# Forming two of sixteen weight residuals per column tile by an accumulating GpSimd DMA instead of VectorE

## Chip, core and metric

One NeuronCore of a Trainium2 chip runs the whole program in one launch. The metric is device microseconds of that core, the median over runs.

## What is computed

One block of a streaming encoder for 256 tokens of width 2048, in float32: a SwiGLU feed-forward (FFN) part, a mixer (a gated linear recurrence beside causal pooling), and a second FFN part, each with an RMS norm before and after it. The change touches only the gate and up products of the two FFN parts:

```python
def swiglu(h, w_gate, w_up, w_down):
    return (jax.nn.silu(h @ w_gate) * (h @ w_up)) @ w_down

h = swiglu(rmsnorm(x, ffn1_pre_g[l]), ffn1_w_gate[l], ffn1_w_up[l], ffn1_w_down[l])
x = x + 0.5 * rmsnorm(h, ffn1_post_g[l])
```

w_gate and w_up are 2048 x 5632, w_down is 5632 x 2048.

## The kernel before, in words

Every product is made of three float32r products, so as to come near float32: an operand a is split into hi = a rounded to float32r, and lo = a - hi, and a·w is taken as a_hi·w_hi + a_hi·w_lo + a_lo·w_hi. These are the three matmuls of the helper `three` (lines 729 to 731). The activations stay on chip in both parts (`xT_hi`, `xT_lo`); the weights stream in once from HBM.

**The stream of weight halves.** A half is 128 x 1024 float32 (512 KB). All weights of the program are one numbered sequence of 640 halves. SP loads two halves (1 MB) at a time into one of four places of `raw` (line 170). For each half ScalarE rounds `raw` into `whi` (function `hi`, line 299), and VectorE subtracts that from `raw` into `wlo` (function `lo`, line 481). `whi` and `wlo` are rings of four halves. TensorE then runs twelve 512-column matmuls on the half (`narrow_half`, line 733).

**What orders it.** Each engine has its own program, written out by hand, and counting semaphores between them. `hi` of half g waits until TensorE is through with half g-4 (`w_used`), since they share a ring place. `lo` of half g waits for `hi_ready` of half g. TensorE waits for `lo_ready` of half g, which counts up in order, one for each half. SP refills a place of `raw` when `lo_ready` shows that both of its halves have been split. GpSimd's queue does small things only: inverse roots, constants for the mixer, and the loads of `gpost`, `gn_sb` and `wp_sb`.

**The column tiles.** The gate and up products of an FFN part are made in eleven column tiles of 512 columns, `up_tile` on each engine: halves 0 to 7 are the gate weights (one half is two 128-row chunks of 512 columns), halves 8 to 15 the up weights. Tile 0 is written out apart, tiles 1 to 10 are a hardware loop. In them ScalarE and VectorE work three halves ahead of TensorE (`AHEAD`). TensorE transposes the hidden tile made before it in front of half 3 (eight short matmuls, line 801), and ScalarE and VectorE split it at their step 4; ScalarE takes the silu of the gate columns at its step 8 (line 348), VectorE multiplies by the up columns behind step 15 (line 520). The down products, the mixer's input product and its output product use the same stream and are not changed.

Of the kernel before, what the change touches and what calls it, by code (L numbers as in the profile page):

```python
# [16 lines left out]
P = 128  # L17
# [4 lines left out]
NT = 512  # L22
# [10 lines left out]
RAW = 4  # L33
# [13 lines left out]
G_FFN1, G_MIX, G_FFN2, LB0, LB1, PSC = 0, 16, 32, 48, 56, 64  # L47
VROWS = 72
VEARLY = G_MIX


TB = (4, 5, 6)
# [3 lines left out]
def build(nc, x_d, g1pre_d, w1g_d, w1u_d, w1d_d, g1post_d, mixpre_d, win_d, lb_d, gnorm_d,  # L56
# [58 lines left out]
    with ExitStack() as ctx:  # L115
        ps = [ctx.enter_context(nc.psum_tensor(f"ps{i}", [P, NT], f32)) for i in range(8)]

        def sem(name):
            return ctx.enter_context(nc.semaphore(name))

        raw_in = [sem(f"raw_in{i}") for i in range(RAW)]
        hi_ready, lo_ready = sem("hi_ready"), sem("lo_ready")
        w_used = sem("w_used")
        x_in = [sem(f"x_in{i}") for i in range(DN)]
        vec_in, vrest_in, gain_in, mixw_in = sem("vec_in"), sem("vrest_in"), sem("gain_in"), sem("mixw_in")
        ident_ok, consts_ok = sem("ident_ok"), sem("consts_ok")
# [91 lines left out]
        def _(pool):  # L218
# [22 lines left out]
            def load_gain(b, gain):  # L241
                pool.wait_ge(w_used, b)
                pool.dma_start(gpost[:], gain[0:1, :].broadcast_to([P, D])).then_inc(gain_in, 16)

            inv_root(0, False)
            load_gain(D1, g1post_d)
            inv_root(1, True)

# [34 lines left out]
            load_gain(OUT, mixpost_d)  # L283
            inv_root(3, False)
            inv_root(4, False)
            load_gain(D2, g2post_d)
            inv_root(5, True)

# [2 lines left out]
        def _(act):  # L291
            def hi(g, j=0):

                if isinstance(j, int) and g + 16 * j >= END:
                    return
                act.wait_ge(raw_in[g // 2 % RAW], j * 32 + 16 * (g // 2 // RAW + 1))
                if not (isinstance(j, int) and g + 16 * j < RING):
                    act.wait_ge(w_used, j * 16 + (g - RING + 1))
                nc.scalar.activation(whi[:, g % RING, :], raw[:, g // 2 % RAW, 1024 * (g % 2):1024 * (g % 2 + 1)],  # L299
                                     ACT.Copy).then_inc(hi_ready, 1)  # L300

            squares = {x_sq: 0, y_sq: 0}
            before = []
# [31 lines left out]
            def up_tile(b, j):  # L335
                f, k, step = (0, 0, 0) if b == U1 else (1, 4, 2)
                first = isinstance(j, int)
                for h in range(16):
                    if first and 6 <= h < 6 + DN:
                        x_square(k, step, h - 6)  # L340
                    if not first and h == 4:
                        hidden_hi(f, j - 1)
                    if h == (13 if first else 8):
                        act.wait_ge(w_used, j * 16 + (b + 8))
                        if first:
                            act.wait_ge(r_ok, k + 1)
                        for t in range(TOK):
                            nc.scalar.activation(nat[:, t, :], ps[t][:], ACT.Silu,  # L348
                                                 scale=rr[:, k, t:t + 1]).then_inc(silu_ok, 1)
                    hi(b + h + AHEAD, j)  # L350
                    if first and h < KC // 2 - 2:
                        x_hi_part(step, G_FFN2 if f else G_FFN1, h + 2)

# [112 lines left out]
        def _(dve):  # L466
# [38 lines left out]
            def up_tile(b, j):  # L505
                f, k, step = (0, 0, 0) if b == U1 else (1, 4, 2)
                first = isinstance(j, int)
                for h in range(16):
                    if first and h == 11:
                        mean_square(k, x_sq, TOK * DN * (step + 1))  # L510
                    if not first and h == 4:
                        hidden_lo(f, j - 1)
                    lo(b + h + AHEAD, j)
                    if first:
                        x_after_half(step, 3, G_FFN2 if f else G_FFN1, h)

                dve.wait_ge(w_used, j * 16 + (b + 16))
                for t in range(TOK):
                    dve.wait_ge(silu_ok, j * 2 + (2 * FTILES * f + t + 1))
                    V.scalar_tensor_tensor(out=nat[:, t, :], in0=ps[2 + t][:], scalar=rr[:, k, t:t + 1],  # L520
                                           in1=nat[:, t, :], op0=ALU.mult, op1=ALU.mult).then_inc(h_ok, 1)
# [202 lines left out]
        def _(pe):  # L724
# [87 lines left out]
            def up_tile(b, j):  # L812
                f, step = (0, 0) if b == U1 else (1, 2)
                first = isinstance(j, int)
                for h in range(16):
                    if not first and h == 3:
                        hidden(f, j - 1)
                    if first and h < 8:
                        x_before_half(step, h)
                    if first and not f and h == 1:  # L820
                        n = VROWS - VEARLY
                        pe.wait_ge(vrest_in, 64)
                        nc.tensor.transpose(ps[3][:, 0:n], vrest[0:n, :], ident[0:n, 0:n]).then_inc(vcol_tr, 1)
                    if first and not f and h == 8:
                        pe.wait_ge(vcol_ok, 2)
                    if h == 0 and (f or not first):
                        pe.wait_ge(silu_ok, j * 2 + 2 * FTILES * f)
                    if h == 8 and (f or not first):
                        pe.wait_ge(h_ok, j * 2 + 2 * FTILES * f)
                    narrow_half(b + h, j, h % 8, ps[0:2] if h < 8 else ps[2:4])  # L830

            def up(b):
# [143 lines left out]
```

## Time and profile before

| what | value |
|---|---|
| median of 3 timed runs | 1878.26 us (1876.82 to 1879.6) |
| profiled execution, first to last instruction (span) | 1875.8 us |
| TensorE matmuls / weight loads busy | 98% / 81% of the span |
| VectorE / ScalarE / GpSimd busy | 51% / 43% / 3% |
| chain of work that ended last | 97% on TensorE |
| DMA | 344.68 MB, mean 184 GB/s |
| mean granted TensorE clock | 0.994 |

The profile gives the span of the execution it recorded, and no other time of it; the median of the timed runs lies 2.5 us above that span, which is taken as what lies around it. Names: PE is TensorE, PEld its weight loads, DVE VectorE, ACT ScalarE, POOL GpSimd, SP the engine that issues the loads. Matmuls overlap each other: one takes 0.39 us, and the next starts 0.23 us after it, so busy time is the time in which at least one is running. The granted clock is a share of 2.4 GHz.

### The profile page before, as it was taken

What the parts mean: (1) busy time and instruction counts of PE and PEld (TensorE: products, weight loads), DVE (VectorE), ACT (ScalarE), POOL (GpSimd) and SP (SyncE); (2) the same over time, 40 slices, a digit from 0 to 9 for tenths busy, and PEclk for the clock granted to TensorE, in tenths of its full rate; (3) what the DMA queues carried; (4) which work ended last, traced back from release to release, by engine and by line L of the source; (5) the groups of instructions that cost most, each with busy time, mean ns of one, the idle gap of its engine ahead of it and who ended that gap; (6) DMA issues with size and microseconds to landing.
All of it is one profiled execution on the core that took longest, in us unless ns stands there. A gap on an engine that the chain in (4) does not pass through costs nothing.

```text
span 1875.8 us, 21635 instructions
## 1 busy us (share of the span) xinstructions
PE 1837.3 (98%) x8386; PEld 1525.8 (81%) x8386; DVE 951.9 (51%) x965; ACT 804.5 (43%) x926; POOL 49.6 (3%) x110
## 2 busy tenths in 40 slices
PE   7999999999999999999999999999999999999997
PEld 6888888888788887788888877888888888788886
DVE  4544445544444444655745456445444544444544
ACT  5444444444433434643234445444444444433432
POOL 0000000000000000250000000000000000000000
PEclk9999999999999999999999999999999999999998
DMA  7665656556566656455443554555555655555552
GB/s 263 189 198 180 196 183 192 188 186 194 194 198 191 197 186 199 158 184 176 135 135 131 200 185 149 188 191 189 183 197 182 198 179 191 208 185 201 186 194 90
DMA packets 145438, 344.68 MB, mean 184 GB/s; under 512 B 5400, under 2 KB 5472, under 8 KB 145008
## 3 DMA queue, kind: packets, MB, share of 16 engines
q1 hardware_dynamic: 144544, 339.77, 55.4%
q0 software_dynamic: 736, 4.26, 0.6%
q8 instruction: 30, 0.49, 0.1%
q14 instruction: 16, 0.13, 0.0%
q10 hardware_dynamic: 112, 0.03, 0.0%
HBM read 341.94 MB, written 2.10 MB: 183 GB/s over the span
## 4 chain that ended last, share of the span: by engine, by line
PE 97%; DVE 1%; ACT 1%; POOL 0%; issue 0%; DMA 0%; DVEq 0%; SPq 0%; POOLq 0%; ACTq 0%; PEldq 0%
PE ps L729 31%; PE ps L731 31%; PE ps L730 31%; PE ps L801 1%; PE ps L891 1%; PE ps L783 1%; DVE x L562 0%; PE ps L928 0%; ACT ps L311 0%; DMA x<-in_x_dram 0%; POOL hrr L282 0%; PE ps L918 0%; PE ps L879 0%; DVE xT_lo L488 0%; ACT xT_hi L318 0%
## 5 line engine op out<-in xcount | busy, mean ns | idle before, releaser
L481 DVE TENSOR_TENSOR wlo<-raw,whi 128x1024 fp32r<-128x1024 f32 x640 | 783.0, 1226 | 844.3 <-ACT whi L299 840.3
L299 ACT ACTIVATE whi<-raw 128x1024 fp32r<-128x1024 f32 x640 | 677.7, 1060 | 919.8 <-PE ps L731 918.8
L729 PE MATMUL ps<-whi,xT_hi 128*128 128x512 f32 x1728 | 680.5, 394 | 6.7 <-DVE wlo L481 4.4
L731 PE MATMUL ps<-whi,xT_lo 128*128 128x512 f32 x1728 | 674.9, 391 | 0.0
L730 PE MATMUL ps<-wlo,xT_hi 128*128 128x512 f32 x1728 | 674.6, 390 | 0.0
L729 PEld LDWEIGHTS ps<-whi,xT_hi 128*128 128x128 f32 x1728 | 325.8, 189 | 73.8 <-issue 4.8
L731 PEld LDWEIGHTS ps<-whi,xT_lo 128*128 128x128 f32 x1728 | 325.7, 188 | 68.7
L730 PEld LDWEIGHTS ps<-wlo,xT_hi 128*128 128x128 f32 x1728 | 326.1, 189 | 66.1
L729 PE MATMUL ps<-whi,hT_hi 128*128 128x512 f32 x832 | 324.5, 390 | 2.0 <-PEq L936 1.6
L731 PE MATMUL ps<-whi,hT_lo 128*128 128x512 f32 x832 | 323.7, 389 | 0.0
L730 PE MATMUL ps<-wlo,hT_hi 128*128 128x512 f32 x832 | 323.7, 389 | 0.0
L729 PEld LDWEIGHTS ps<-whi,hT_hi 128*128 128x128 f32 x832 | 156.2, 188 | 36.4 <-DVE yg L534 2.3
L731 PEld LDWEIGHTS ps<-whi,hT_lo 128*128 128x128 f32 x832 | 156.2, 188 | 32.7
L730 PEld LDWEIGHTS ps<-wlo,hT_hi 128*128 128x128 f32 x832 | 156.2, 188 | 31.9
L348 ACT ACTIVATE nat<-ps,rr 128x512 f32<-128x512 f32 x44 | 27.9, 686 | 33.2 <-PE ps L731 33.2
L520 DVE SCALAR_TENSOR_TENSOR nat<-ps,rr,nat 128x512 f32<-128x512 f32 x44 | 31.0, 747 | 10.8 <-PE ps L731 10.8
L318 ACT ACTIVATE xT_hi<-ps,vcol 128x256 fp32r<-128x256 f32 x48 | 19.9, 472 | 36.5 <-PE ps L783 36.5
L488 DVE SCALAR_TENSOR_TENSOR xT_lo<-ps,vcol,xT_hi 128x256 fp32r<-128x256 f32 x48 | 20.8, 478 | 23.3 <-ACT xT_hi L318 23.3
L801 PE MATMUL ps<-ident,nat 128*128 128x128 f32 x208 | 27.0, 273 | 3.2 <-DVE nat L520 3.2
L801 PEld LDWEIGHTS ps<-ident,nat 128*128 128x128 f32 x208 | 24.1, 140 | 7.2 <-DVE nat L520 4.1
L501 DVE TENSOR_TENSOR hT_lo<-ps,hT_hi 128x512 f32 (+1 forms) x44 | 28.2, 682 | 2.8 <-ACT hT_hi L332 2.8
L783 PE MATMUL ps<-ident,x 128*128 128x128 f32 x96 | 16.0, 301 | 11.9 <-DVE x L562 8.6
(99 smaller groups left out, 365.7 us busy)
## 6 DMA issues: line engine op xcount, KB each, us to landing
raw<-in_ffn_w_gate_dram SPq DMA_DIRECT2D x88, 1024.0 KB, 5.2
raw<-in_ffn_w_up_dram SPq DMA_DIRECT2D x88, 1024.0 KB, 5.2
raw<-in_ffn_w_down_dram SPq DMA_DIRECT2D x88, 1024.0 KB, 5.2
raw<-in_w_in_dram SPq DMA_DIRECT2D x40, 1024.0 KB, 5.1
raw<-in_w_out_dram SPq DMA_DIRECT2D x16, 1024.0 KB, 4.9
x<-in_x_dram SPq DMA_DIRECT2D x4, 512.0 KB, 9.3
gpost<-in_ffn_post_g_dram POOLq DMA_DIRECT2D x2, 1024.0 KB, 5.0
out_dram<-x SPq DMA_DIRECT2D x4, 512.0 KB, 2.9
```

The source lines that it names most:

```text
L299: nc.scalar.activation(whi[:, g % RING, :], raw[:, g // 2 % RAW, 1024 * (g % 2):1024 * (g % 2 + 1)], ACT.Copy).then_inc(hi_ready, 1)
L318: ins = nc.scalar.activation(xT_hi[:, k, :], ps[TB[s % 3]][:, c * SEQ:(c + 1) * SEQ], ACT.Copy, scale=vcol[:, g0 + k:g0 + k + 1])
L348: nc.scalar.activation(nat[:, t, :], ps[t][:], ACT.Silu, scale=rr[:, k, t:t + 1]).then_inc(silu_ok, 1)
L481: V.tensor_tensor(wlo[:, g % RING, :], raw[:, g // 2 % RAW, 1024 * (g % 2):1024 * (g % 2 + 1)], whi[:, g % RING, :].bitcast(f32), ALU.subt ...
L488: ins = V.scalar_tensor_tensor(out=xT_lo[:, k, :], in0=ps[TB[s % 3]][:, c * SEQ:(c + 1) * SEQ], scalar=vcol[:, g0 + k:g0 + k + 1], in1=xT_ ...
L501: V.tensor_tensor(flat(hT_lo[:, bass.ds(j * 4 + 2 * c, 2), :]), ps[4 + c][:], flat(hT_hi[:, bass.ds(j * 4 + 2 * c, 2), :]).bitcast(f32), A ...
L520: V.scalar_tensor_tensor(out=nat[:, t, :], in0=ps[2 + t][:], scalar=rr[:, k, t:t + 1], in1=nat[:, t, :], op0=ALU.mult, op1=ALU.mult).then_ ...
L729: mm(bank, a_hi, whi[:, s, c0:c0 + NT], start=start, stop=False)
L730: mm(bank, a_hi, wlo[:, s, c0:c0 + NT], start=False, stop=False)
L731: return mm(bank, a_lo, whi[:, s, c0:c0 + NT], start=False, stop=stop)
L783: ins = nc.tensor.transpose(ps[TB[s % 3]][:, c * SEQ + t * P:c * SEQ + (t + 1) * P], x[:, t, k * P:(k + 1) * P], ident[:])
L801: ins = nc.tensor.transpose(ps[banks[c]][:, q * SEQ + t * P:q * SEQ + (t + 1) * P], src[:, t, n:n + P], ident[:])
```

## The change

In tiles 1 to 10 of both FFN parts halves 5 (gate) and 13 (up) get their lo part in another way. ScalarE, having rounded `raw` into `whi`, also writes the negative of the rounded value into `wlo` (a second ACTIVATE of the same size, scale -1). GpSimd waits for that (`neg_ok`) and issues a DMA that reads the same 512 KB of weights from HBM once more and adds them to `wlo` where they land (`accum_op`). VectorE does nothing on these halves but keep the count: it waits for `neg_ok` and for its own earlier count, and adds one to `lo_ready`. TensorE waits for the DMA (`acc_in`) in front of these halves. That is 2 halves x 10 tiles x 2 parts = 40 halves of 640.

```diff
+BY_DMA = (5, 13)
...
+            def residual_halves(b, wg, wu):
+                f = 0 if b == U1 else 1
+                for j in range(1, FTILES):
+                    for m, (h, w) in enumerate(zip(BY_DMA, (wg, wu))):
+                        c = 2 * (h % 8)
+                        rows = w[0].rearrange("(c p) f -> p c f", p=P)
+                        dst = wlo[:, (b + h) % RING, :].rearrange("p (c f) -> p c f", c=2)
+                        pool.wait_ge(neg_ok, j * 2 + (2 * (FTILES - 1) * f + m - 1))
+                        pool.dma_start(dst, rows[:, c:c + 2, bass.ds(j * NT, NT)],
+                                       accum_op=ALU.add).then_inc(acc_in, 16)
+
             inv_root(0, False)
+            residual_halves(U1, w1g_d, w1u_d)
             load_gain(D1, g1post_d)
...
             inv_root(4, False)
+            residual_halves(U2, w2g_d, w2u_d)
...
+            def hi_and_minus(g, j):
+
+                hi(g, j)
+                nc.scalar.activation(wlo[:, g % RING, :], raw[:, g // 2 % RAW, 1024 * (g % 2):1024 * (g % 2 + 1)],
+                                     ACT.Copy, scale=-1.0).then_inc(neg_ok, 1)
...
-                    hi(b + h + AHEAD, j)
+                    if not first and h + AHEAD in BY_DMA:
+                        hi_and_minus(b + h + AHEAD, j)
+                    else:
+                        hi(b + h + AHEAD, j)
...
-                    lo(b + h + AHEAD, j)
+                    if not first and h + AHEAD in BY_DMA:
+                        m = BY_DMA.index(h + AHEAD)
+                        dve.wait_ge(neg_ok, j * 2 + (2 * (FTILES - 1) * f + m - 1))
+                        dve.wait_ge(lo_ready, j * 16 + (b + h + AHEAD))
+                        dve.sem_inc(lo_ready, 1)
+                    else:
+                        lo(b + h + AHEAD, j)
...
+                    if not first and h in BY_DMA:
+                        pe.wait_ge(acc_in, j * 32 + (32 * (FTILES - 1) * f + 16 * BY_DMA.index(h) - 16))
                     narrow_half(b + h, j, h % 8, ps[0:2] if h < 8 else ps[2:4])
```

Two places of the programs that result. First ScalarE in the column loop, around the rounding of half 13. Before (line 299 is `hi`):

```order
L298 REGISTER_ALU [waits raw_in2]
L299 ACTIVATE whi<-raw 128x1024 [waits w_used]
L298 REGISTER_ALU [waits raw_in3]
L299 ACTIVATE whi<-raw 128x1024 [waits w_used]
```

After (line 316 is `hi`, line 322 the negative):

```order
L315 REGISTER_ALU [waits raw_in2]
L316 ACTIVATE whi<-raw 128x1024 [waits w_used]
L322 ACTIVATE wlo<-raw 128x1024
L315 REGISTER_ALU [waits raw_in3]
L316 ACTIVATE whi<-raw 128x1024 [waits w_used]
```

The second ACTIVATE stands between the rounding of half 13 and that of half 14; all else keeps its place. Second TensorE in the same loop, at the seam between half 4 and half 5 (lines 761 to 763 are the three matmuls of `three`). Before:

```order
L729 MATMUL ps<-whi,xT_hi 128x512
L730 MATMUL ps<-wlo,xT_hi 128x512
L731 MATMUL ps<-whi,xT_lo 128x512
L735 REGISTER_ALU
L729 MATMUL ps<-whi,xT_hi 128x512 [waits lo_ready]
L730 MATMUL ps<-wlo,xT_hi 128x512
```

After:

```order
L761 MATMUL ps<-whi,xT_hi 128x512
L762 MATMUL ps<-wlo,xT_hi 128x512
L763 MATMUL ps<-whi,xT_lo 128x512
L863 ISA
L767 REGISTER_ALU [waits acc_in]
L761 MATMUL ps<-whi,xT_hi 128x512 [waits lo_ready]
L762 MATMUL ps<-wlo,xT_hi 128x512
```

A wait for the DMA now stands in front of the half's first matmul, beside the old one for `lo_ready`. On GpSimd the 20 DMAs of each FFN part stand one behind another, each with its wait, and nothing but them until the load of `gpost`:

```order
L239 TENSOR_TENSOR rr<-ms,mhalf 128x2 [waits ms_ok,gp]
L257 DMA wlo<-in_ffn_w_gate_dram 128x2x512 [waits neg_ok]
L257 DMA wlo<-in_ffn_w_up_dram 128x2x512 [waits neg_ok]
L257 DMA wlo<-in_ffn_w_gate_dram 128x2x512 [waits neg_ok]
L257 DMA wlo<-in_ffn_w_up_dram 128x2x512 [waits neg_ok]
```

Where the root (line 239) was followed by the load of `gpost`, the accumulating DMAs now stand between them.

## Rows read from the trace of the kernel before

**Rows 1.** The page, part 1: busy us, share of the span, instructions.

```profile
PE 1837.3 (98%) x8386; PEld 1525.8 (81%) x8386; DVE 951.9 (51%) x965; ACT 804.5 (43%) x926; POOL 49.6 (3%) x110
```

**Rows 2.** Waits of PE: engine, line <- releaser: us in total, times, longest us.

```profile
PE ps L729 <- DVE wlo L481: 4.4, 1, 4.4
...
PE ps L801 <- DVE nat L520: 3.2, 2, 1.6
```

**Rows 3.** Windows, column tiles 1 to 10: us, busy (x) by engine, clock, DMA share, GB/s.

```profile
100.00:500.00 400.00, 400.00 (x1802) 331.93 (x1802) 199.13 (x180) 171.94 (x180) 0.00 (x0) 1.00 0.59 189
```

**Rows 4.** Lines by form: busy us, mean ns, idle before and its releaser.

```profile
L481 DVE TENSOR_TENSOR wlo<-raw,whi 128x1024 fp32r<-128x1024 f32 x640 | 783.0, 1226 | 844.3 <-ACT whi L299 840.3 <-DMA gpost<-in_ffn_post_g_dram 2.2 <-DVE T L618 0.3
...
L299 ACT ACTIVATE whi<-raw 128x1024 fp32r<-128x1024 f32 x640 | 677.7, 1060 | 919.8 <-PE ps L731 918.8 <-DMA raw<-in_ffn_w_gate_dram 0.8
```

**Rows 5.** Timeline of ACT, halves 5 and 6: start us, us, what, idle before.

```profile
288.84 1.06 ACT L299 ACTIVATE whi<-raw 128x1024 fp32r<-128x1024 f32 x1 [1.66 <-PE ps L731]
291.56 1.06 ACT L299 ACTIVATE whi<-raw 128x1024 fp32r<-128x1024 f32 x1 [1.66 <-PE ps L731]
```

**Rows 6.** Timeline of ACT, halves 13 and 14.

```profile
311.49 1.06 ACT L299 ACTIVATE whi<-raw 128x1024 fp32r<-128x1024 f32 x1 [1.66 <-PE ps L731]
314.21 1.06 ACT L299 ACTIVATE whi<-raw 128x1024 fp32r<-128x1024 f32 x1 [1.66 <-PE ps L731]
```

**Rows 7.** Timeline of PE: half 5's first, two within half 11, half 13's first.

```profile
297.69 0.39 PE L729 MATMUL ps<-whi,xT_hi 128*128 128x512 f32 x1
...
314.46 0.39 PE L731 MATMUL ps<-whi,xT_lo 128*128 128x512 f32 x1
314.69 0.39 PE L729 MATMUL ps<-whi,xT_hi 128*128 128x512 f32 x1
...
319.45 0.39 PE L729 MATMUL ps<-whi,xT_hi 128*128 128x512 f32 x1
```

**Rows 8.** Timeline of SP's queue: refills of raw after halves 5 and 13.

```profile
291.18 0.37 SPq L170 DMA_DIRECT2D raw<-in_ffn_w_up_dram  x1
...
313.97 0.37 SPq L170 DMA_DIRECT2D raw<-in_ffn_w_gate_dram  x1
```

**Rows 9.** DMA issues: line, op, xcount, KB each, median us to landing.

```profile
raw<-in_ffn_w_gate_dram SPq DMA_DIRECT2D x88, 1024.0 KB, 5.2
...
gpost<-in_ffn_post_g_dram POOLq DMA_DIRECT2D x2, 1024.0 KB, 5.0
...
wp_sb<-in_w_pool_dram POOLq DMA_DIRECT2D x1, 1024.0 KB, 6.1
...
gn_sb<-in_hgrn_g_norm_dram POOLq DMA_DIRECT2D x1, 64.0 KB, 3.4
```

**Rows 10.** Windows around the refill issued at 313.97 (columns as in rows 3).

```profile
314.40:314.90 0.50, 0.50 (x3) 0.40 (x3) 0.00 (x0) 0.50 (x1) 0.00 (x0) 1.00 0.00 0
314.90:315.40 0.50, 0.50 (x4) 0.40 (x3) 0.10 (x1) 0.37 (x1) 0.00 (x0) 1.00 1.24 98
...
318.40:318.90 0.50, 0.50 (x4) 0.42 (x3) 0.50 (x1) 0.00 (x0) 0.00 (x0) 1.00 0.26 98
318.90:319.40 0.50, 0.50 (x4) 0.42 (x3) 0.35 (x1) 0.00 (x0) 0.00 (x0) 1.00 0.00 0
```

**Rows 11.** Timeline of PE: two gaps outside the column loops.

```profile
507.10 1.09 PE L801 MATMUL ps<-ident,nat 128*128 128x128 f32 x8 [1.61 <-DVE nat L520]
...
752.53 1.27 PE L783 MATMUL ps<-ident,x 128*128 128x128 f32 x8 [4.46 <-DVE x L562]
```

**Rows 12.** Windows right behind these two gaps.

```profile
755.00:756.00 1.00, 0.98 (x2) 0.83 (x3) 1.00 (x3) 0.73 (x1) 0.00 (x0) 0.50 1.03 389
507.00:508.00 1.00, 0.90 (x9) 0.90 (x9) 0.04 (x1) 0.21 (x1) 0.00 (x0) 1.00 0.86 176
```

**Rows 13.** Chain of waits behind the second gap: start us, us, what.

```profile
758.37 0.43 PE ps L730
758.80 0.43 PE ps L731
```

More of the change, by code:

```diff
@@ L123, in build @@
         w_used = sem("w_used")
+        neg_ok, acc_in = sem("neg_ok"), sem("acc_in")
         x_in = [sem(f"x_in{i}") for i in range(DN)]
```

## The prediction

> **What bounds the kernel now.** I read the busy shares first. TensorE runs matmuls for 98% of the span, VectorE is at 51%, ScalarE at 43% [rows 1]. The 400 us stretch that holds most of the first part's column tiles shows the same more sharply: TensorE is busy for 400.00 of 400.00 us, at the full granted clock, while VectorE works for 199 us of it [rows 3]. The waits say so from the other side. In the whole program TensorE waited once for a lo part, 4.4 us, when the stream started, and its next wait for VectorE is the hidden tile at the two ends of the up products, 3.2 us in sum [rows 2]; neither is in the part changed here. So in the loop that the change edits nothing ever arrives late at TensorE. VectorE's idle time ahead of the lo subtraction, 844 us, ends almost always with ScalarE's rounding, and ScalarE's 920 us ends with TensorE giving a ring place free [rows 4]: both helpers are paced by TensorE, and their idle time is slack.
>
> The question is therefore not what the change takes off VectorE. It is how much slack the lo part of a half has, and whether the new way of making it fits in.
>
> **The slack of the two halves.** ScalarE starts rounding half 13 at 311.49 and half 14 at 314.21 [rows 6]; the step of 2.72 us is TensorE's time for one half. TensorE begins half 13 at 319.45 [rows 7]. For half 5 the two times are 288.84 [rows 5] and 297.69 [rows 7]; this one has 0.9 us more, since TensorE does its eight transposes in between. So the time from the rounding's start to the use is 7.96 us for half 13 and 8.85 us for half 5. Today rounding (1.06) and subtraction (1.23) take about 2.3 us of it [rows 4].
>
> **What is removed.** 40 subtractions of 1.226 us [rows 4], 49 us of VectorE's time. All of it lies beside matmuls, so it is worth nothing on the path: TensorE is the cover, and it does not idle there.
>
> **What is added on ScalarE.** 40 ACTIVATEs of the same size as the rounding, 1.06 us each, 42 us [rows 4]. The negative of half 13 starts when the rounding ends, at 312.55, and ends at 313.61; half 14 is rounded from 314.21 on, so 0.6 us is left [rows 6]. For half 5 it ends at 290.96, ahead of 291.56 [rows 5]. The idle time of 1.66 us before each rounding hides it; without that cover it would delay the next half's parts, which themselves have over 5 us of slack. Cost: nothing.
>
> **What is added on VectorE and moved on SP's queue.** Two waits and a count, no data. VectorE gets to the next subtraction long before ScalarE has rounded that half. The count for half 13 now comes at 313.6, where the subtraction had it ready just ahead of the refill of `raw` at 313.97; for half 5 the refill stood at 291.18, the count now comes at 290.96 [rows 8]. So the refill goes out some 0.2 to 0.3 us earlier, and at the same moment as the new DMA. The refill itself isn't needed until ScalarE rounds the same place's next halves, seven halves after half 13 was rounded, 17 us after the issue, against 5.2 us to land [rows 9]. Even a landing twice as late is hidden.
>
> **What is added on GpSimd.** Its queue does nothing in these stretches (0.00 busy in 400 us) [rows 3], so no DMA there waits behind another, and what stands behind them, the load of `gpost`, has its own wait for the end of the up products. Cost: nothing.
>
> **The added wait, which is the price.** TensorE may not start half 13 until the accumulating DMA has landed. What is queued behind that wait is every later matmul. The DMA goes out at about 313.61 and TensorE wants it at 319.45, so it has 5.8 us; for half 5, from 290.96 to 297.69, 6.7 us [rows 5 to 7]. No row shows a DMA that adds. The nearest rows: the smallest copy that GpSimd issues, 64 KB, lands 3.4 us after the issue; its copies of 1 MB land after 5.0 us (long rows) and 6.1 us (1 KB rows); SP's 1 MB in the same 2 KB rows as here after 5.2 us [rows 9]. So a plain copy of 512 KB, alone, would come in between 3.4 and 5.2 us, in time for both.
>
> But it is neither plain nor alone. The refill goes out with it. Alone, the refill moves no data for its first 1.0 us, then moves for 3.6 us (314.9 to 318.5) at a DMA share near 1, and lands 0.6 us later [rows 10, 9]. While it moves, the 16 DMA engines are full, so the two share them. The new DMA has 256 rows of 2 KB, the refill 512; taken in turns, the new one is through when 256 rows of each have gone. And an addition in place has to fetch two inputs for each row, the weights and what lies in `wlo`; I count its rows double. That makes 0.5 MB of refill and 1 MB for the addition, 1.5 times 3.6 = 5.4 us of moving. Landing: 1.0 + 5.4 + 0.6 = **7.0 us** after the issue.
>
> The bounds: 3.4 us from below (the smallest copy), and 9.7 us from above, the slowest copy of 1 MB, 6.1 us, behind a whole refill, 3.6 us. I take 7.0, which is near neither end but is the one that counts the work.
>
> The Trainium skill (Collectives: The Full Stack, "The bandwidth ceiling: the fold count and why AG ≠ RS ≠ AR") says that a reducing DMA runs at half a copy's rate, because it needs two source reads and not because of the addition; no run so far shows that here. By it the sum would stay as it is.
>
> **The sum.** Half 13: 313.61 + 7.0 - 319.45 = 1.16 us late, times 20 = 23 us. Half 5: 290.96 + 7.0 - 297.69 = 0.27 us, times 20 = 5 us. A late half is not caught up: the ring ahead is measured from TensorE's own progress, so each tile pays again. Together 28 us on the span of 1875.8, that is 1904; the median of the runs lies 2.5 us above the span, so **1906 us**. At the upper bound, 9.7 us, the halves are 3.86 and 2.97 us late, 137 us in all, and the time is 2015.
>
> **The rivals.** Changes of under 0.2%, 3.8 us here, can't be told from none by a measurement of this kernel.
>
> *The DMA lands in time* (not slower). The mechanism: the addition costs no more engine time than a copy. Then the moving takes 0.5 MB + 0.5 MB, 3.6 us, and the landing comes after 5.2 us, ahead of 5.8. It decides at 5.8 us; up to 6.0 the loss stays under 3.8 us. Time 1878, between 1876 and 1882. For it: copies of twice the size land in 4.6 to 5.2 us mostly alone. Against it: the second input and the refill that always goes out together with it. The skill's fit for DMAs that GpSimd issues (DMA: Bandwidth & Descriptors, "Anatomy of one DMA — SWDGE (gpsimd) path"), 2.0 us plus the bytes at 436 GB/s, makes 3.2 us by estimate for 512 KB. By it this rival would win; the rows for 1 MB, 5.0 and 6.1 us against its 4.4 [rows 9], say that it is low here even without an addition.
>
> *The addition is much slower than two reads* (over 9.7 us). If each row costs four times a copy's: 2 MB + 0.5 MB, 9.0 us of moving, landing after 10.6 us; halves 4.8 and 3.9 us late, 173 us. On top the clock: behind a gap of 1.61 us TensorE kept its full clock, behind one of 4.46 us it was granted half [rows 11, 12], and matmuls then stepped by 0.43 instead of 0.23 us [rows 13, 7] for some 5 us, which loses up to 2.6 us each time, 50 to 100 us. Time 2100 to 2150. For it: nothing in this trace bounds the pace of an addition.
>
> *TensorE speeds up* (faster). It steps by 0.227 us (2.72 over twelve matmuls) where 512 columns at 2.4 GHz need 0.213. If that difference were VectorE's traffic beside it, 40 halves of 12 matmuls would gain 6.6 us: 1872. Against it: in a window with VectorE at 0.00 [rows 10] it still steps by 0.23 us [rows 7], and ScalarE gets nearly the same traffic in exchange.
>
> That the change doesn't happen is out: the 40 DMAs stand in GpSimd's program.
>
> **How the numbers follow.** A landing between 6.0 and 9.7 us, the forecast: 0.62. In time: 0.20; I don't make it less, since 5.8 us and my 7.0 lie close and the sharing is argued, not seen. Over 9.7 us: 0.15. Faster: 0.03. So faster 0.03, same 0.20, slower 0.77. The range goes from 1876, the in-time case, to 2015, the upper bound; what it leaves out is the slow addition and the faster case, under 0.2.
>
> **What would show it.** In the profile after, VectorE's busy time falls by 49 us and ScalarE's rises by 42. TensorE's waits get a new row, on the DMA into `wlo`, 20 to 40 times, about 28 us, longest near 1.2 us, and more before half 13 than before half 5. The list of DMA issues gets 40 of 512 KB with a landing near 7 us, and the refill beside them lands later than 5.2 us. The clock stays at 1.00 in the loops. I am wrong if the landing is under 5.8 us or the wait row is missing; wrong in size if the landing is past 9 us; and wrong in mechanism if TensorE waits for anything else there.

## The result, and the profile after

| what | before | after |
|---|---|---|
| median of 4 timed runs each | 1878.93 us | 1992.96 us (1990.8 to 1994.52) |
| span of the profiled execution | 1875.8 us | 1992.8 us |
| mean granted TensorE clock | 0.994 | 0.982 |

The ratio is 1.061, with a 95% interval from 1.060 to 1.062. The kernel is 114 us slower. The forecast was 1906 us with a range from 1876 to 2015. The sign was right, and so was the place of the loss, a DMA that lands late in front of halves 5 and 13. The size was not, 28 us against 114, and two parts of the loss, the fall of the clock and the restart behind each gap, were not in the forecast at all.

Two lines of the page of the changed kernel, to be set against [rows 1]: busy times, and the DMA queue that GpSimd feeds (packets, MB, share of 16 engines' span).

```profile
PE 1873.5 (94%) x8386; PEld 1540.7 (77%) x8386; DVE 903.0 (45%) x925; ACT 842.1 (42%) x966; POOL 97.8 (5%) x150
...
q0 software_dynamic: 11616, 25.23, 6.4%
```

VectorE lost the 49 us that were taken off it (951.9 to 903.0), ScalarE got 38 us more. TensorE does the same matmuls and is busy 36 us longer, which the forecast had nowhere. GpSimd's queue of DMAs moved 21 MB more (it had 4.26 MB).

The waits of TensorE, against [rows 2] (engine, line <- releaser: us in total, times, longest us):

```profile
PE ps L761 <- DMA wlo<-in_ffn_w_up_dram: 34.1, 13, 3.3
PE ps L761 <- DMA wlo<-in_ffn_w_gate_dram: 30.4, 20, 2.0
PE ps L761 <- DVE wlo L507: 21.2, 8, 4.4
```

The first two rows are new. The third had 4.4 us before; the other 16.8 us are the same gaps, put down to VectorE's last subtraction where the profile couldn't place the DMA. Together the gaps make 30.4 + 34.1 + 16.8 = 81.3 us. With the 36.2 us of busy time that is 117.5, and the span grew by 117.0. So the whole loss is there. Idle time is not all of the lateness, though: the last matmul before a gap still runs for 0.39 us, where the next would have started 0.23 us after it. So a half is 0.16 us later than its idle time says, 88 us over the 40 gaps; the other 6.4 us of it are counted as busy time.

The landings, against [rows 9] (KB each, median us from issue to landing):

```profile
raw<-in_ffn_w_gate_dram SPq DMA_DIRECT2D x88, 1024.0 KB, 5.3
...
wlo<-in_ffn_w_gate_dram POOLq DMA_DIRECT2D x20, 512.0 KB, 8.1
wlo<-in_ffn_w_up_dram POOLq DMA_DIRECT2D x20, 512.0 KB, 8.2
```

The addition lands 8.1 to 8.2 us after its issue, and not after 7.0. The gate row of `raw` is a median over 88 loads, of which only 20 go out beside an addition, so it doesn't say what the refill pays. The loads that do go out beside one, taken one by one in the first part, land after 5.6 us behind half 5 and 5.7 us behind half 13 (medians of ten), where the same loads took 5.2 and 5.15 us before: 0.4 to 0.6 us later.

One half 13 from its rounding to its use, from the timelines of ScalarE, GpSimd, SP's queue and TensorE (start us, us, what, idle before):

```profile
343.85 1.06 ACT L316 ACTIVATE whi<-raw 128x1024 fp32r<-128x1024 f32 x1 [1.66 <-PE ps L763]
344.82 1.04 ACT L322 ACTIVATE wlo<-raw 128x1024 fp32r<-128x1024 f32 x1
...
346.16 1.20 POOL L257 DMA_DIRECT2D wlo<-in_ffn_w_up_dram  x1 [23.06 <-ACT wlo L322]
...
346.11 6.04 SPq L174 DMA_DIRECT2D raw<-in_ffn_w_gate_dram  x2
...
354.46 0.49 PE L761 MATMUL ps<-whi,xT_hi 128*128 128x512 f32 x1 [2.48 <-DMA wlo<-in_ffn_w_up_dram]
```

ScalarE starts the rounding at 343.85, so TensorE wants the half 7.96 us later, at 351.81. The negative is done at 344.82 + 1.04 = 345.86. GpSimd's DMA starts at 346.16, 0.30 us later; the refill had gone out at 346.11 (its row joins two issues, the second at 351.8). TensorE starts at 354.46, 2.65 us late, of which 2.48 us are idle. Half 5 of the same tile is 1.5 us late in the same way (wanted at 328.43, started at 329.93). Over all 40 the lateness is 2.7 us in front of half 13 and 1.7 us in front of half 5.

What the DMA engines did in that stretch, in windows (columns as in [rows 3]; the last two numbers are the DMA share and the GB/s):

```profile
349.40:349.90 0.50, 0.50 (x4) 0.42 (x3) 0.00 (x0) 0.50 (x1) 0.00 (x0) 1.00 1.04 406
349.90:350.40 0.50, 0.50 (x4) 0.42 (x3) 0.01 (x1) 0.45 (x1) 0.00 (x0) 1.00 1.04 369
...
351.40:351.90 0.50, 0.50 (x3) 0.15 (x1) 0.21 (x1) 0.00 (x0) 0.00 (x0) 1.00 1.19 221
351.90:352.40 0.50, 0.07 (x1) 0.00 (x0) 0.00 (x0) 0.39 (x1) 0.00 (x0) 1.00 1.09 201
...
352.90:353.40 0.50, 0.00 (x0) 0.00 (x0) 0.30 (x1) 0.17 (x1) 0.00 (x0) 1.00 1.13 209
```

At 349.4 to 350.4 the engines move data at the pace of a plain load, 369 to 406 GB/s. By 350.9 the 1 MB of the refill is through: the eight windows from 346.9 to 350.9, not all shown, add up to 0.98 MB. Then come 2 us at 201 to 221 GB/s with the engines just as full. That is the addition, at half the pace. The queues settle whose data it is: q1 is the one that SP feeds, q0 GpSimd's (packets, MB, share of the engines). First the refill's landing, then 350.1 to 350.9, then 351.9 to 352.9:

```profile
raw<-in_ffn_w_gate_dram SPq DMA_DIRECT2D x1, 1024.0 KB, 5.7
```

```profile
q1 hardware_dynamic: 131, 0.27, 97.1%
```

```profile
q0 software_dynamic: 99, 0.20, 110.1%
```

In the first of these stretches every packet is the refill's, in the second every one is the addition's. The first packet of the addition starts 4.7 us after its issue (4.6 us for half 5, medians of 20). So in the changed kernel the two transfers weren't served in turns: the refill went first, and the addition used the engines after it.

### The profile page after: what moved, and what is told of

The parts are those of the page before. It is cut to its first block, busy times and chain, and to the rows that moved or that the text cites. A ratio compares the mean times of both kernels' runs of the same rounds, so it can differ in the third digit from the quotient of the medians.

```text
span 1992.8 us, 21735 instructions
## 1 busy us (share of the span) xinstructions
PE 1873.5 (94%) x8386; PEld 1540.7 (77%) x8386; DVE 903.0 (45%) x925; ACT 842.1 (42%) x966; POOL 97.8 (5%) x150
## 4 chain that ended last, share of the span: by engine, by line
PE 79%; DMA 14%; ACT 3%; issue 3%; DVE 2%; POOL 0%; DVEq 0%; SPq 0%; POOLq 0%; ACTq 0%; PEldq 0%
PE ps L761 26%; PE ps L763 25%; PE ps L762 25%; DMA wlo<-in_ffn_w_gate_dram 8%; DMA wlo<-in_ffn_w_up_dram 5%; ACT wlo L322 2%; PE ps L925 1%; PE ps L815 1%; DVE wlo L507 1%; ACT whi L316 0%; DVE x L594 0%; PE ps L833 0%; PE ps L962 0%; ACT ps L334 0%; DMA x<-in_x_dram 0%
## 5 line engine op out<-in xcount | busy, mean ns | idle before, releaser
L507 DVE TENSOR_TENSOR wlo<-raw,whi 128x1024 fp32r<-128x1024 f32 x600 | 734.0, 1226 | 1009.1 <-ACT whi L316 1005.3
L761 PE MATMUL ps<-whi,xT_hi 128*128 128x512 f32 x1728 | 694.4, 402 | 87.7 <-DMA wlo<-in_ffn_w_up_dram 34.1
L763 PE MATMUL ps<-whi,xT_lo 128*128 128x512 f32 x1728 | 684.9, 396 | 0.0
L762 PE MATMUL ps<-wlo,xT_hi 128*128 128x512 f32 x1728 | 684.5, 396 | 0.0
L761 PEld LDWEIGHTS ps<-whi,xT_hi 128*128 128x128 f32 x1728 | 331.2, 192 | 172.4 <-DVE wlo L507 56.5
L763 PEld LDWEIGHTS ps<-whi,xT_lo 128*128 128x128 f32 x1728 | 331.2, 192 | 71.1
L762 PEld LDWEIGHTS ps<-wlo,xT_hi 128*128 128x128 f32 x1728 | 331.8, 192 | 67.2
L257 POOL DMA_DIRECT2D wlo<-in_ffn_w_gate_dram x20 | 24.3, 1216 | 479.2 <-ACT wlo L322 479.2
L257 POOL DMA_DIRECT2D wlo<-in_ffn_w_up_dram x20 | 24.1, 1203 | 468.2 <-ACT wlo L322 468.2
L322 ACT ACTIVATE wlo<-raw 128x1024 fp32r<-128x1024 f32 x40 | 41.6, 1041 | 0.0
```

What stands on the lines that cost most here:

```text
L257: pool.dma_start(dst, rows[:, c:c + 2, bass.ds(j * NT, NT)], accum_op=ALU.add).then_inc(acc_in, 16)
L322: nc.scalar.activation(wlo[:, g % RING, :], raw[:, g // 2 % RAW, 1024 * (g % 2):1024 * (g % 2 + 1)], ACT.Copy, scale=-1.0).then_inc(neg_ok, 1)
L507: V.tensor_tensor(wlo[:, g % RING, :], raw[:, g // 2 % RAW, 1024 * (g % 2):1024 * (g % 2 + 1)], whi[:, g % RING, :].bitcast(f32), ALU.subt ...
L761: mm(bank, a_hi, whi[:, s, c0:c0 + NT], start=start, stop=False)
L762: mm(bank, a_hi, wlo[:, s, c0:c0 + NT], start=False, stop=False)
L763: return mm(bank, a_lo, whi[:, s, c0:c0 + NT], start=False, stop=stop)
```

## Experiments

The theory from this profile was A: the addition waits for the refill that goes out beside it, and its late landing is the whole loss, directly and by the clock. The rival was B: an accumulating DMA takes some 5 us from issue to first data whatever runs beside it. A second rival was that the added traffic or ScalarE's added work slow the loop by themselves.

**The refill held back.** SP's refills that would go out beside an addition wait for it, 38 of the 40; the two behind half 13 of the last tile of each part are not held (the loop over tiles is written out for it):

```diff
+                if hold:
+                    sp.wait_ge(acc_in, 16 * hold)
                 dst = raw[:, n % RAW, :].rearrange("p (c f) -> p c f", c=chunks)
                 sp.dma_start(dst, src).then_inc(raw_in[n % RAW], 16)
```

> The changed kernel, but SP waits with the refill of raw that would go out beside each accumulating DMA until that DMA has landed (38 of the 40). In the changed kernel the DMA lands 8.1 us after its issue and moves data only in the last 3. Theory A (the refill's packets are served first, and the addition starts when they are through): the landing falls to about 5 us (1.2 us to start, 3 us of data, 0.6), TensorE's waits for it vanish, time about 1880. Theory B (an accumulating DMA needs some 5 us from its issue to its first data, whatever runs beside it): the landing stays near 8 us and the time near 1993.

Measured: 1897.99 us, ratio 1.011 (1.009 to 1.013). The list of DMA issues, the gate row:

```profile
wlo<-in_ffn_w_gate_dram POOLq DMA_DIRECT2D x20, 512.0 KB, 6.0
```

The landing fell from 8.1 to 6.0 us, so B is out as it was stated, and 95 of the 114 us went with it. But it is 6.0 and not the 5 that A gave. The windows behind a DMA issued at 316.72 show where the rest lies:

```profile
317.72:318.22 0.50, 0.50 (x4) 0.42 (x3) 0.00 (x0) 0.48 (x1) 0.20 (x1) 1.00 0.00 0
...
318.72:319.22 0.50, 0.50 (x4) 0.39 (x3) 0.50 (x1) 0.00 (x0) 0.00 (x0) 1.00 1.01 98
...
320.72:321.22 0.50, 0.50 (x4) 0.41 (x3) 0.27 (x1) 0.20 (x1) 0.00 (x0) 1.00 1.11 205
...
321.72:322.22 0.50, 0.50 (x4) 0.35 (x2) 0.46 (x1) 0.00 (x0) 0.00 (x0) 1.00 0.41 70
```

No data until 318.2, then 1.7 us in which the pace climbs, then 205 GB/s at a full DMA share to about 321.9, landing at 322.7. The addition's first packet starts 1.9 us after the issue, where the refill's data started after 1.0 us [rows 8, 10]. So A is right about the refill, and some of B is true too: the addition by itself is slower to begin and moves at half a load's pace. Of the 20 us that are left, 5.9 are the idle time of the two gaps whose refill wasn't held (3.5 and 2.5 us); no other gap in front of half 13 is over 0.54 us.

**Halves 4 and 12 in place of 5 and 13.** The refills then go out half a step away from the additions:

```diff
-BY_DMA = (5, 13)
+BY_DMA = (4, 12)
```

> The changed kernel with halves 4 and 12 in place of 5 and 13. The place in the ring and the slack are the same (7.96 us and 8.85 us), but the refill goes out 2.7 us before the addition instead of beside it, and the next one 2.7 us after it. Theory A: the addition waits for the rest of one refill only, lands after 5 to 6 us, little or no waiting, 1880 to 1895. Theory B: landing near 8 us, time near 1993.

Measured: 1901.77 us, ratio 1.013 (1.011 to 1.014).

```profile
wlo<-in_ffn_w_gate_dram POOLq DMA_DIRECT2D x20, 512.0 KB, 5.9
wlo<-in_ffn_w_up_dram POOLq DMA_DIRECT2D x20, 512.0 KB, 6.4
```

5.9 and 6.4 us without any wait added on SP: just moving the addition away from the refill's issue does nearly as much as holding the refill. The upper end of A's range was 1895; the time is 7 us above it. The addition alone was underrated here as well, and the one for half 12 has a refill 1.4 us ahead of it, so that its first packet starts 2.9 us after its issue and not 1.9. One gap, in the last tile of the first part, is 2.8 us long and has a fall of the clock behind it.

**A plain copy in its place, refill beside it.** The residual of these halves is left out of the computation.

```diff
-                        pool.dma_start(dst, rows[:, c:c + 2, bass.ds(j * NT, NT)],
-                                       accum_op=ALU.add).then_inc(acc_in, 16)
+                        pool.dma_start(dst, rows[:, c:c + 2, bass.ds(j * NT, NT)]).then_inc(acc_in, 16)
```

> The changed kernel with a plain copy of the same rows in place of the addition; wlo of these halves then holds the weights and not their residual, so the addition is left out of the computation. Theory A: the copy also starts behind the refill, at about 4.9 us, moves for 1.6 us and lands after 6.5 to 6.7 us; half 13 is still 1.1 us late and half 5 is not, time about 1900. Theory B (the delay belongs to accumulating): landing at 3.5 to 5 us, no waiting, time 1880.

Measured: 1901.10 us, ratio 1.012 (1.010 to 1.014). The landings, and TensorE's waits for it:

```profile
wlo<-in_ffn_w_gate_dram POOLq DMA_DIRECT2D x20, 512.0 KB, 6.3
wlo<-in_ffn_w_up_dram POOLq DMA_DIRECT2D x20, 512.0 KB, 6.5
```

```profile
PE ps L760 <- DMA wlo<-in_ffn_w_up_dram: 15.9, 20, 1.1
```

This is A's number, 6.3 to 6.5 us and 1901. The copy's first packet starts 4.1 to 4.2 us after its issue, and the refill beside it lands after 5.25 us, as without company. Even without adding, 512 KB from GpSimd beside a refill comes too late for half 13 (20 waits, 15.9 us), and in time for half 5.

**All the added work, but no early wait.** The negative and the addition go to a spare tile, VectorE subtracts as before, TensorE waits two halves later:

```diff
-                        dst = wlo[:, (b + h) % RING, :].rearrange("p (c f) -> p c f", c=2)
+                        dst = spare[:].rearrange("p (c f) -> p c f", c=2)
...
-                    if not first and h in BY_DMA:
-                        pe.wait_ge(acc_in, j * 32 + (32 * (FTILES - 1) * f + 16 * BY_DMA.index(h) - 16))
+                    if not first and h - 2 in BY_DMA:
+                        pe.wait_ge(acc_in, j * 32 + (32 * (FTILES - 1) * f + 16 * BY_DMA.index(h - 2) - 16))
```

> All added work stays (the negative on ScalarE, the 40 accumulating DMAs, the refill beside them), but goes to a spare tile, VectorE makes the lo parts as before, and TensorE waits for the DMA two halves (5.4 us) later. The residuals come from VectorE, so nothing is left out. If the whole loss of 114 us is the late landing and what follows from it: 1880, landing still 8.1 us. If added traffic, descriptors or ScalarE's work slow the loop by themselves: above 1885.

Measured: 1878.38 us, ratio 1.000 (0.999 to 1.001). Landings, and the two longest waits of TensorE:

```profile
spare<-in_ffn_w_gate_dram POOLq DMA_DIRECT2D x20, 512.0 KB, 6.9
spare<-in_ffn_w_up_dram POOLq DMA_DIRECT2D x20, 512.0 KB, 6.2
...
PE ps L814 <- DVE x L593: 8.6, 2, 4.5
PE ps L760 <- DVE wlo L508: 4.4, 1, 4.4
```

Both waits are in [rows 2] or outside the loops, as before. Traffic, descriptors and ScalarE's 42 us cost nothing; the loss is the wait alone. One number came out otherwise: the landing is 6.9 and 6.2 us here, and not 8.1, because VectorE's subtraction now follows the negative and so the refill goes out 1.1 to 1.2 us after the addition (315.67 against 314.46 in this trace). With that head start the addition begins 1.9 us after its issue, as it does alone, and here it is the refill that is late: 7.7 us behind half 5 and 7.5 behind half 13 to land. It is needed 17 us after its issue, so this costs nothing.

**One half at a time.** Half 13 alone, and half 5 alone, by DMA (the counts of the semaphores follow):

```diff
-BY_DMA = (5, 13)
+BY_DMA = (13,)
```

> The changed kernel with half 13 alone by DMA; half 5 goes back to VectorE. Theory: each of the 20 stalls costs by itself, 2.65 us of lateness and about 0.2 us to restart, and the fall of the granted clock comes after these longer gaps: 57 us plus about 14 half-clock stretches of 3.4 us (24 us), 1959. Rival: the clock falls only because two gaps follow each other within each tile; then it stays up here and the time is about 1936.

> The changed kernel with half 5 alone by DMA; half 13 goes back to VectorE. Gaps of 1.5 us: 20 times 1.5 plus 0.2 to restart, 34 us, and no fall of the clock: 1912. The sum of this loss and that of half 13 alone should give the 114 us of the change. Under the rival for the clock both are cheaper than that, and the sum falls short by some 24 us.

Measured: half 13 alone 1953.33 us, ratio 1.040 (1.038 to 1.041); half 5 alone 1914.57 us, ratio 1.019 (1.018 to 1.021), where 1959 and 1912 were expected. TensorE's waits and the mean clock, half 13 alone, then half 5 alone:

```profile
PE ps L761 <- DMA wlo<-in_ffn_w_up_dram: 29.6, 11, 3.5
PE ps L761 <- DVE wlo L507: 26.3, 10, 4.4
...
core 0: 1952.8 us, clock 0.983
```

```profile
PE ps L761 <- DMA wlo<-in_ffn_w_gate_dram: 29.5, 20, 2.0
...
core 0: 1914.2 us, clock 0.992
```

The losses are 75 and 36 us, together 111 of the 114. Each gap costs by itself. The clock tells them apart: with the 1.5 us gaps alone its mean is 0.992 (before 0.994), with the 2.5 us gaps alone 0.983. Gap by gap, it fell to half behind one of the 20 of half 5, the first and longest with 2.03 us, and behind 11 of the 20 of half 13 (all 20 are 2.4 to 3.5 us long). No fall at all was expected for half 5. A mean of 0.983 over 1952.8 us means 33 us of full-speed work lost, against 11 us before. The rival that needed both gaps in a tile is out.

**The negative first.** ScalarE writes the negative, then the rounded half, so the DMA goes out earlier by one ACTIVATE:

```diff
-                hi(g, j)
+                act.wait_ge(raw_in[g // 2 % RAW], j * 32 + 16 * (g // 2 // RAW + 1))
+                act.wait_ge(w_used, j * 16 + (g - RING + 1))
                 nc.scalar.activation(wlo[:, g % RING, :], raw[:, g // 2 % RAW, 1024 * (g % 2):1024 * (g % 2 + 1)],
                                      ACT.Copy, scale=-1.0).then_inc(neg_ok, 1)
+                nc.scalar.activation(whi[:, g % RING, :], raw[:, g // 2 % RAW, 1024 * (g % 2):1024 * (g % 2 + 1)],
+                                     ACT.Copy).then_inc(hi_ready, 1)
```

> The changed kernel with ScalarE writing the negative first and the rounded half second, so that the DMA goes out 1.0 us earlier; nothing else moves. If the loss is the path from the free ring place to the landing, each of the 40 gaps gets 1.0 us shorter (2.65 to 1.65, 1.5 to 0.5) and the clock no longer falls, since the gaps are then all under 1.7 us: 1878 + 20 x (1.65 + 0.5) + 40 x 0.2 = 1929. If what counts were the DMA's traffic, nothing would change: 1993.

Measured: 1934.60 us, ratio 1.030 (1.028 to 1.032).

```profile
PE ps L764 <- DMA wlo<-in_ffn_w_up_dram: 22.0, 20, 3.0
PE ps L764 <- DMA wlo<-in_ffn_w_gate_dram: 20.5, 20, 1.6
...
wlo<-in_ffn_w_gate_dram POOLq DMA_DIRECT2D x20, 512.0 KB, 8.5
wlo<-in_ffn_w_up_dram POOLq DMA_DIRECT2D x20, 512.0 KB, 7.6
```

One us earlier took 58 us off, which is what a path of latency does and a matter of bandwidth doesn't. The clock is back at 0.993: of the 40 gaps only the one of 2.99 us, in a part's last tile, has a fall behind it. The gains are unequal. In front of half 5 the idle time went from 30.4 to 20.5 us, so only 0.5 of the 1.0 us was kept; in front of half 13 it went from 50.9 to 22.0, more than was expected. In lateness that is 14 us above the expectation for half 5 and 8 below it for half 13, which makes the 6 us between 1929 and 1935.

The refill goes out 0.76 us behind the addition of half 5 and 0.90 us behind that of half 13, and it doesn't get ahead any more. For the addition issued at 187.19 (half 13), the refill's landing, then the packets of 192 to 193 by queue:

```profile
raw<-in_ffn_w_gate_dram SPq DMA_DIRECT2D x1, 1024.0 KB, 8.1
```

```profile
q0 software_dynamic: 64, 0.13, 70.4%
q1 hardware_dynamic: 64, 0.13, 39.2%
```

Here the two are served in turns, packet for packet, and it is the refill that lands last, after 8.1 us. A packet of the addition takes 1.8 times as long as one of the refill. By itself the refill's data starts 1.0 us after its issue and the addition's 1.9. With the refill 0.90 us behind, the addition's first packet does come at 1.9 us, and the refill's at 2.3. With it 0.76 us behind, the refill is a little ahead, and the addition's first packet comes only at 3.6 us, after which the two take turns again. So in these traces the one whose data begins first has the engines to itself for a while. Why the other doesn't join in at once, the traces don't say.

**Both together.** Negative first and refill held:

> Negative first and the refill held back until the DMA has landed. Landing 6.0 us after the issue, issue 1.3 us after the rounding place is free, 7.3 us against a slack of 7.96 and 8.85: in time, 1878 to 1880, the same as the kernel before. If some other cost of the addition were left, it would show here as more than 1882.

Measured: 1885.18 us, ratio 1.004 (1.002 to 1.005). The forecast of 1878 to 1880 failed by 5 us, and the waits say where:

```profile
PE ps L773 <- DMA wlo<-in_ffn_w_up_dram: 4.8, 2, 2.7
```

38 of the 40 gaps are gone. The two left, 2.1 and 2.7 us, each have a fall of the clock behind them. They are in the last tile of each part, where the refill behind half 13 belongs to the down product and wasn't held. **Held there as well:**

```diff
+                        hold = {D1: 20, D2: 40}.get(b, 0) if i == 0 and n == 4 else 0
-                        load(b + len(order) * i + n, rows[:, order[n]:order[n] + 2, 1024 * i:1024 * (i + 1)], 2)
+                        load(b + len(order) * i + n, rows[:, order[n]:order[n] + 2, 1024 * i:1024 * (i + 1)], 2, 0, hold)
```

> As the run with the negative first and the refill held (1885), but the two refills that were not held there, the ones behind half 13 of the last tile of each part, are held too. In that run TensorE waited for the addition twice, 2.7 and 2.1 us, just there, and the clock fell twice. Theory: these two are all of its 7 us; the time is now that of the kernel before, 1878, the interval around a ratio of 1.000. If adding work beside TensorE costs anything by itself, some us stay.

Measured: 1877.90 us, ratio 1.000 (0.999 to 1.001). Busy times of the page, and the landing:

```profile
PE 1837.1 (98%) x8386; PEld 1525.9 (81%) x8386; DVE 902.9 (48%) x925; ACT 842.3 (45%) x966; POOL 97.8 (5%) x150
...
wlo<-in_ffn_w_gate_dram POOLq DMA_DIRECT2D x20, 512.0 KB, 5.8
```

TensorE is busy for the same 1837 us as before the change [rows 1], VectorE has its 49 us less, and the time is that of the kernel before. This version makes the change harmless. Nothing points to one that would beat both, since the work taken off VectorE was never on the path.

**The addition by itself.** Refill held, first a plain copy of the same rows (the residual of these halves is left out), then the addition on half the columns:

> The held refill (negative second) with a plain copy in place of the addition; the residual of these halves is left out of the computation. This is the same transfer without adding and without company, to set against 6.0 us with adding. A plain copy has one input a row: 1.5 us of data where the addition has 3 to 3.4, and GpSimd issues it in 0.7 us where the addition takes 1.2. Expected landing 3.6 to 4.2 us, 1878 to 1880.

> The held refill (negative second) with only the first 512 columns of each half by the addition (256 KB), the rest by VectorE. With 6.0 us for 512 KB at about 205 GB/s: 1.3 to 1.7 us less, a landing of 4.3 to 4.7 us. If the time were set by a fixed delay and not by the bytes, the landing would stay above 5.5.

Measured: 1880.97 us (ratio 1.0015, 1.0005 to 1.0025) and 1879.51 us (1.001, 1.000 to 1.002). The landings, copy of 512 KB, then addition of 256 KB:

```profile
wlo<-in_ffn_w_gate_dram POOLq DMA_DIRECT2D x20, 512.0 KB, 3.9
```

```profile
wlo<-in_ffn_w_gate_dram POOLq DMA_DIRECT2D x20, 256.0 KB, 4.1
```

Without company, 512 KB land after 3.9 us copied and 5.8 to 6.0 us added; 256 KB added take 4.1. So the addition costs 2.1 us more than the copy, and its second half 1.9 us. The halved pace, 205 against 400 GB/s, makes 1.3 us of either, and the longer issue most of the rest: GpSimd's instruction takes 1.20 us for the addition, 0.71 for the copy and 0.87 for the addition of 256 KB. That is 1.7 of the 2.1 us and 1.6 of the 1.9; what is left wasn't traced to anything. The 256 KB came in a little under the 4.3 to 4.7 expected. The copy's 1881 is 1 us above the 1880 expected: TensorE still waited for it twice, 1.1 and 0.8 us, in the two last tiles, where the refill isn't held.

## Why the prediction was right and wrong

*What bounds the kernel, what is removed and added on VectorE, ScalarE and GpSimd:* right. The run with all the work and no early wait has the time of the kernel before.

*The slack, 7.96 and 8.85 us:* right, the late halves start where these numbers and the landing put them. One reading ahead of it was incomplete: TensorE's longest wait for VectorE isn't the hidden tile's 3.2 us but 8.6 us, twice, ahead of the transposes of `x`. It lies outside the loops, so nothing hung on it:

```profile
PE ps L783 <- DVE x L562: 8.6, 2, 4.5
```

*Sign, place and the main mechanism:* right. TensorE waits for the addition in front of halves 5 and 13, more in front of 13, and the loss repeats in every tile.

*The size:* wrong, in three terms of the sum.

- **The landing in "The added wait, which is the price".** It was 7.0 us and measured 8.1 to 8.2. The part for the transfer alone was put at 1.0 + 3.6 + 0.6 = 5.2 us and is 5.8 to 6.0. Counting the addition's rows double was right: it moves at 205 GB/s where a load moves at 400. The start was wrong, taken from SP's load, 1.0 us, where GpSimd's addition has its first packet after 1.9. The step "taken in turns" failed for this kernel: it let the refill's packets cost the addition 1.8 us by interleaving, and the queues show the refill through first, with the addition's first packet at 4.6 to 4.7 us; with the refill held back the landing falls by 2.1 us. Turns do happen with the negative first, where the addition has 0.9 us of head start. Beside it stood a hand-over of 0 us from ScalarE to GpSimd that measures 0.3. Together 1.4 us on a path of which only 1.16 and 0.27 us were to stick out, so the mean lateness went to 2.7 and 1.7 us: 88 us and not 28. The lateness is a small difference between two large numbers, and 20% on the one trebled it.
- **The clock, left at 1.00 for gaps of this size.** The forecast had one gap of 1.61 us without a fall and one of 4.46 with it, and charged the clock only to the rival beyond 9.7 us. Of the changed kernel's 40 gaps, the 18 of 1.25 to 1.82 us have no fall behind them, and 14 of the 22 of 1.96 to 3.33 us have one. Two gaps in front of half 13, and the matmuls behind the second:

```profile
153.34 0.49 PE L761 MATMUL ps<-whi,xT_hi 128*128 128x512 f32 x1 [2.37 <-DVE wlo L507]
...
304.02 0.49 PE L761 MATMUL ps<-whi,xT_hi 128*128 128x512 f32 x1 [2.50 <-DMA wlo<-in_ffn_w_up_dram]
304.35 0.40 PE L762 MATMUL ps<-wlo,xT_hi 128*128 128x512 f32 x1
304.59 0.39 PE L763 MATMUL ps<-whi,xT_lo 128*128 128x512 f32 x1
```

The clock in windows behind the first of them (153.34) and behind the second (304.02):

```profile
153.00:158.00 5.00, 4.66 (x21) 3.86 (x21) 0.84 (x2) 1.06 (x1) 0.00 (x0) 1.00 0.49 186
...
306.00:307.00 1.00, 1.00 (x4) 0.81 (x3) 0.00 (x0) 0.00 (x0) 0.00 (x0) 0.50 0.06 23
307.00:308.00 1.00, 1.00 (x4) 0.72 (x4) 0.00 (x0) 0.00 (x0) 0.00 (x0) 0.50 0.00 0
```

Behind the first it stays at 1.00, behind the second it is at half for some 3 us. By the mean clock, 0.982 of 1992.8 us against 0.994 of 1875.8, the change loses 36 - 11 = 25 us this way. The count agrees: in the 5 us behind those 14 gaps the mean clock is 0.66, and 14 x 5 x 0.34 = 24 us. The Trainium skill (TensorE: Matmul & The Clock Gate, "What's actually happening") has an idle TensorE fall back to half its clock. The trace agrees: half is what the windows show.
- **The restart, not counted.** Behind a gap the first matmul is 0.33 us ahead of the next instead of 0.23, as the timeline above shows, and takes 0.49. Where the clock stays up, the eighth start behind the first comes after 1.94 us instead of 1.81. So a gap costs 0.13 us more, 5 us for the 40.

The three terms, 88 + 25 + 5, make 118 us, and the span grew by 117. The first is confirmed by the runs that shorten or remove the gaps. The other two are read from the trace and agree with the busy time (25 + 5 + the 6.4 us of the last matmuls, against 36.2), but no run takes one away and leaves the gaps.

That 1993 lies in the range of 1876 to 2015 is in part luck. The upper end stood for a landing after 9.7 us; by the forecast's own sum a landing after 8.15 us gives 1876 + 2.5 + 20 x (2.31 + 1.42) = 1953. The other 40 us are the hand-over of 0.3 us, 12 us in all, the clock and the restart, which the range didn't contain.

*The refill would land later than 5.2 us:* right, but by little, 5.6 to 5.7 us, since it goes first. In turns from the start it would have been much later; the 8.0 to 8.3 us with the negative first show that.

*The clock stays at 1.00 in the loops, the longest wait near 1.2 us:* wrong, by the terms above. The longest wait is 3.3 us.

*The rivals:* the landing in time didn't come, though a held refill and an earlier issue bring it about together. The estimate of 3.2 us for 512 KB from the Trainium skill's fit (DMA: Bandwidth & Descriptors, "Anatomy of one DMA — SWDGE (gpsimd) path") is low against the 3.9 us of the plain copy without company and far from the 8.1 of the addition beside a refill. The slow addition, over 9.7 us, didn't come, but its clock term did, from shorter gaps. TensorE didn't speed up: in the version with all refills held, with VectorE's 49 us gone and no gap left, it is busy for 1837.1 us against 1837.3. The Trainium skill (Collectives: The Full Stack, "The bandwidth ceiling: the fold count and why AG ≠ RS ≠ AR") has a reducing DMA run at half a copy's rate because it reads two sources. The 205 against 400 GB/s here agree with the half; the reason wasn't tested.

## What to carry to other kernels

Where a kernel's bound engine never waits, taking work off another engine can't gain, and the only number that matters is the slack of what replaces it: from the place being free to the last byte landed, beside whatever else is triggered by the same event. When that path and the slack come within a us of each other, price the loss at both bounds, with the clock's fall included, and not at the middle. If such a transfer must be used, issue it first thing and keep the bulk loads from going out with it; here an order of two instructions and a held load were worth 115 us.

## What was not expected of the hardware

- A 1 MB load issued by SP at the same moment as a 512 KB addition issued by GpSimd is through first and loses only 0.4 to 0.6 us (5.6 to 5.7 us against 5.2), while the addition lands 2.1 us later, its first packet 4.6 to 4.7 us after its issue instead of 1.9. With the load 0.90 us behind, the two go in turns, packet for packet, and land after 8.1 us (load) and 7.6 us (addition). With it 1.1 to 1.2 us behind, they land after 7.5 to 7.7 and after 6.2 to 6.9 us. So a shift of 1 us in who is issued first turns the order round.
- Adding in a DMA costs 2.1 us on 512 KB over a plain copy (5.8 to 6.0 against 3.9), by half the data pace and a longer issue (1.20 against 0.71 us).
- TensorE's clock fell behind gaps shorter than expected: the shortest with a fall is 1.96 us in the changed kernel and 2.03 us with half 5 alone, while none of the more than 100 gaps up to 1.95 us in front of these halves has one. From there to 2.7 us it goes both ways (no fall behind 8 gaps of 2.33 to 2.56 us in the changed kernel). What decides between two like gaps stays open. Length alone doesn't: at the start of every run here, where TensorE first waits for weights, a gap of 4.4 us has no fall behind it.
